# Sums over partitions by a product with ones, and another order of work at the start of both norms

## The chip, the cores and the metric

The kernel runs on one core of a Trainium2 chip. What is measured is the device time of one execution in microseconds (us), taken as the median of several executions. The engines are named as in the profile: PE (matrix products), ACT, DVE, POOL, and SP, which here only issues DMAs. Each engine works through its own queue in order, and the engines meet at semaphores.

## The reference

Two transformer blocks follow each other on a sequence of 2048 rows of 1024 values.

- Block 1: layer norm of x, product with `w_in` (1024 x 2560), three mixers (a spatial gate, a convolution of width 31, attention in a window of 128), product with `w_out`, a residual and a layer norm.
- Block 2: RMS norm, product with `w_in_2` (1024 x 4096), rotary embedding of queries and keys, three dilated windows of attention mixed by their log-sums, a short convolution, gates, product with `w_out_2`, RMS norm and a residual.

```python
x = layer_norm(x, ln_in_g, ln_in_b);   h = einsum('bsd,de->bse', x, w_in)
ya, yb, yc = spatial_gating(...), conformer_conv(...), window_attention(...)
x = layer_norm(ALPHA * x + concat(ya, yb, yc) @ w_out, post_ln_g, post_ln_b)
h = rmsnorm(x, norm_pre_g_2);          z = einsum('bsd,de->bse', h, w_in_2)
y = concat(dilated_attention(q, k, v) * silu(g), conv(...)) @ w_out_2
x = x + rmsnorm(y, norm_post_g_2)
```

## The kernel before, in words

The products with `w_in` and `w_in_2` are made in float16 with each operand split into a high and a low part, three products per pair (`products`, L164). The normed and transposed input of a block lies in SBUF whole, as `xh` and `xl`. The weights come in chunks of 256 columns: 11 in block 1, 16 in block 2. The class `Weights` (L173) takes a chunk through these steps, with two buffers of each kind:

- `sp_load` (SP): DMA of the chunk into `raw`, once the chunk two before it has been split (`ready`) and read (`read`).
- `act_sum` (ACT, L225): the sum of squares of each partition. The squares themselves are thrown away; they are written into `hi`, and so ACT waits until the chunk two before is spent.
- `pool_scale` (POOL, L230 to L243): the sum over the partitions by `partition_all_reduce`, a maximum, the power -1/2, and the factors made of it.
- Then the split: for the first chunks (`fast`) `act_hi` (L247) and `dve_lo` (L251), for the others `act_scale` (L256) on ACT and `pool_split` (L260, L262) on POOL.

The stages of a block share these weights. `norm_stage` (L286) runs at the start of each block (tag a, tag b) and makes the first three chunks' products. Its 16 row tiles come in four groups g of four. Its order is written out by hand in the list `work`, which every engine walks through: `turn` g is PE's 32 transposes (L439), ACT's scaling out of PSUM (L476), POOL's cast to `xh` (L613) and DVE's `xl` (L565); `scale` g+1 is the fetch of the next four tiles (L370), their moments on DVE (L378), a power on POOL (L427) and the scaling on DVE (L400, L402); `load` n is a chunk's sum and, if it is fast, its split; `group` n g is the product of chunk n with group g, two PSUM banks of it. On SP the load of chunk 2 stands ahead of the fetch of group 1.

For values (`fv` and `n` chunks of the norms) and for queries and keys (`rope_stage`, L1560) a bound on the results is needed too: `dve_bound` reduces the chunk's largest weights (L525, L1613), `pool_bound` (L534, L1621) sums over the partitions, `dve_fit` (L540, L1627) makes the factor that ACT's read of the result waits for. `dve_widest` and `pool_widest` (L406, L410) find the largest gain over all partitions once in each norm.

After the norm, block 1 has `conv_stage` and `spatial_stage`, block 2 has `rope_stage` and `gate_stage` (L1701). In them chunk n+1 is prepared while PE works on chunk n, whose 8 tiles (one PSUM bank each) are numbered m % 8. ACT sums at the chunk's start and scales after one group (conv, spatial) or at m % 8 == 3 (rope, gate). The stages of attention between and after them (`window_stage`, `project_stage`, `dilated_stage`) are not touched. `Banks.take` hands the eight PSUM banks (six in the conv stage) out in turn, and each taker waits for the reader of the last use.

Of the kernel before, what the change touches and what calls it, by code (L numbers as in the profile page):

```python
# [7 lines left out]
FH = mybir.dt.float16  # L8
# [49 lines left out]
def two_block_program(nc, A, out, ctx, stack):  # L58
    pe, act, dve, pool, sp = (Engine(e) for e in (nc.tensor, nc.scalar, nc.vector, nc.gpsimd, nc.sync))
    named, spare, handed, serial = {}, {}, {}, itertools.count()  # L60
    KEPT = ("c_first", "c_rest", "g_set", "w_in0", "w_in1", "a_n", "g_u", "a_w", "d_w", "g_w", "ow0", "ow1")
# [78 lines left out]
    un, us = sb("un", [128, 2, 16]), sb("us", [128, 2, 16])  # L140

    c_first, c_rest, g_set = sem("c_first"), sem("c_rest"), sem("g_set")
    FIRST, REST = (c_first, 48), (c_rest, 128)
    POWER = (g_set, 1)
# [17 lines left out]
    nc.gpsimd.memset(power[:], -0.5).then_inc(*g_set.up())  # L162

# [9 lines left out]
    class Weights:  # L173
# [3 lines left out]
        def __init__(self, tag, scope, w, chunks, block):  # L177
# [9 lines left out]
            self.dma, self.a_n, self.g_u = sems("w_in", 2), sem("a_n"), sem("g_u")  # L187
# [3 lines left out]
            self.scaled = [(self.g_u, self.g_u.n + 7 * n + 7) for n in range(len(chunks))]  # L191
# [28 lines left out]
        def act_sum(self, n):  # L220

            act.wait_ge(*self.landed[n])
            if n > 1:
                act.wait_ge(*self.spent[n - 2])
            nc.scalar.activation(self.hi[n % 2][:], self.raw[n % 2][:], ACT.Square, accum_out=self.size[:, n, 0:1]).then_inc(*self.a_n.up())  # L225

        def pool_scale(self, n):
            one, total, root, by = self.size[:, n, 0:1], self.size[:, n, 1:2], self.size[:, n, 2:3], self.size[:, n, 3:4]
            pool.wait_ge(*self.summed[n])
            nc.gpsimd.partition_all_reduce(total, one, 128, bass.bass_isa.ReduceOp.add).then_inc(*self.g_u.up())  # L230
            pool.wait_ge(*self.g_u.now())
            nc.gpsimd.tensor_scalar(total, total, 1e-30, None, ALU.max).then_inc(*self.g_u.up())
            pool.wait_ge(*self.g_u.now())
# [11 lines left out]
        def act_hi(self, n):  # L245
            act.wait_ge(*self.scaled[n])
            nc.scalar.activation(self.hi[n % 2][:], self.raw[n % 2][:], ACT.Identity, scale=self.size[:, n, 3:4]).then_inc(*self.a_w.up())  # L247
# [10 lines left out]
        def pool_split(self, n):  # L258
            pool.wait_ge(*self.by_act[n])
            nc.gpsimd.tensor_copy(self.hi[n % 2][:], self.raw[n % 2][:]).then_inc(*self.g_w.up())  # L260
# [25 lines left out]
    def norm_stage(tag, scope, src, gain, shift, gain_ready, x_ready, late, xh, xl, keep, wts, outs, heads, ones):  # L286
# [8 lines left out]
        g_pw, g_one, g_bd = sem("g_pw"), sem("g_one"), sem("g_bd")  # L295
        d_bd, d_vs = sem("d_bd"), sem("d_vs")
        vt, vh = heads
        d_wd, d_gs, g_wd, g_xh = sem("d_wd"), sem("d_gs"), sem("g_wd"), sem("g_xh")
# [4 lines left out]
        wts.widened = d_gs.at(2)  # L303
# [2265 lines left out]
```

## Time and profile before

| | us |
|---|---|
| Median of 3 runs (lowest to highest) | 2485.16 (2481.81 to 2493.55) |
| The profiled execution | 2490.25 |
| Its span in the profile | 2488.1 |
| PE busy in the span | 2093.7 (84%) |
| DVE busy | 1439.9 (58%) |
| ACT busy | 900.3 (36%) |
| POOL busy | 892.9 (36%) |

The stages, read from where their lines start and end: norm a 0 to 218, conv 218 to about 504, spatial to about 626, window attention and projection to 1024, norm b to 1241, rope to 1490 on PE, gate to about 1770, then the dilated attention with the last projection. The share of busy time is a mean over these; the waits of one stage are read from its own rows. "issue" as a releaser means that the engine waited for nothing that the profile shows.

### The profile page before, as it was taken

Reading aid. Unit: us, or ns where it says so; the run is one execution under the profiler, and the core shown is the slowest. Engines: PE = TensorE matmul, PEld = TensorE weight load, DVE = VectorE, ACT = ScalarE, POOL = GpSimd, SP = SyncE. Lnnn points to the kernel's source line nnn. Section 1 sums busy time; section 2 is a strip of 40 time slices with the busy share of each in tenths; the row PEclk is TensorE's granted clock in tenths of the full one; section 3 lists DMA queues with packets and bytes.
Section 4 is the critical chain, followed back from the end, with each engine's and each line's share of the span. In section 5 each row is a group of like instructions: output and inputs, shape, how many; then the busy total and the mean of one; then the engine's idle time right before and its main releaser. Section 6 shows DMA issues by size and latency. Waiting matters only on the chain.

```text
span 2488.1 us, 43133 instructions
## 1 busy us (share of the span) xinstructions
PE 2093.7 (84%) x16150; PEld 1540.2 (62%) x16150; DVE 1439.9 (58%) x3510; ACT 900.3 (36%) x1933; POOL 892.9 (36%) x1015
## 2 busy tenths in 40 slices
PE   2789999888588799449899999999787787776898
PEld 1444777777478688349744444747676666665776
DVE  3732877946699444465256774222198888894421
ACT  2322222221578100123223332222088787783111
POOL 2212112145141799322122131222125667873222
PEclk8899999989799899779999999999999988897999
DMA  4333131124860333222244432211267765664443
GB/s 119 111 94 119 51 123 33 45 69 144 207 146 28 127 106 114 93 93 87 73 152 115 131 113 79 68 51 52 71 160 173 171 158 151 153 191 136 144 142 108
DMA packets 285630, 279.93 MB, mean 113 GB/s; under 512 B 39936, under 2 KB 237952, under 8 KB 285168
## 3 DMA queue, kind: packets, MB, share of 16 engines
q1 hardware_dynamic: 279200, 270.01, 37.6%
q0 software_dynamic: 1680, 5.51, 0.6%
q10 hardware_dynamic: 4544, 1.66, 0.4%
q8 instruction: 129, 2.11, 0.4%
q14 instruction: 77, 0.63, 0.1%
HBM read 171.22 MB, written 93.31 MB: 106 GB/s over the span
## 4 chain that ended last, share of the span: by engine, by line
PE 41%; DVE 22%; issue 11%; POOL 11%; DMA 7%; SPq 4%; ACT 3%; DVEq 0%; ACTq 0%; POOLq 0%
PE bank L170 37%; DVE bank L843 4%; DVE s2m L2163 3%; DVE p2l L2169 3%; DMA qr<-qf 2%; SPq L1689 2%; POOL cm L2041 1%; DVE qf L1659 1%; DVE qr L1657 1%; PE bank L439 1%; POOL qs L2209 1%; DVE s2sl L1662 1%; ACT s2sh L1641 1%; POOL kept L2045 1%; POOL kept L2043 1%
## 5 line engine op out<-in xcount | busy, mean ns | idle before, releaser
L2106 PE MATMUL bank<-ident,p2r 128*128 128x128 f32 x900 | 172.0, 306 | 89.9 <-DVE p2l L2169 86.2
L170 PE MATMUL bank<-xh,w2h 128*128 128x512 f16 x640 | 243.3, 380 | 3.6 <-POOL w2l L262 3.6
L170 PE MATMUL bank<-xh,w2l 128*128 128x512 f16 x640 | 243.2, 380 | 0.0
L170 PE MATMUL bank<-xl,w2h 128*128 128x512 f16 x640 | 243.2, 380 | 0.0
L170 PE MATMUL bank<-w2h,xh 128*128 128x256 f16 x768 | 211.2, 275 | 24.9 <-issue 16.7
L170 PE MATMUL bank<-w1h,xh 128*128 128x256 f16 x768 | 214.5, 279 | 10.7 <-DVE s1st L833 10.7
L170 PE MATMUL bank<-w1l,xh 128*128 128x256 f16 x768 | 214.3, 279 | 0.0
L170 PE MATMUL bank<-w1h,xl 128*128 128x256 f16 x768 | 214.0, 279 | 0.0
L170 PE MATMUL bank<-w2l,xh 128*128 128x256 f16 x768 | 211.2, 275 | 0.0
L170 PE MATMUL bank<-w2h,xl 128*128 128x256 f16 x768 | 211.0, 275 | 0.0
L2169 DVE SCALAR_TENSOR_TENSOR p2l<-bank,p2h 128x512 f16<-128x512 f32 (+1 forms) x288 | 164.2, 570 | 48.8 <-ACT p2h L2135 48.3
L2106 PEld LDWEIGHTS bank<-ident,p2r 128*128 128x128 f32 x900 | 103.7, 152 | 138.7 <-DVE p2l L2169 136.8
L843 DVE SCALAR_TENSOR_TENSOR bank<-ain,cw,bank 128x512 f32<-128x512 f32 x240 | 181.2, 755 | 14.2 <-ACT bank L794 7.1
L2163 DVE CUSTOM_DVE_ANT_0 s2m<-bank,both,finv 128x256 f32<-128x256 f32 (+1 forms) x384 | 160.4, 455 | 9.0 <-PE bank L2096 8.7
L2135 ACT ACTIVATE p2h<-bank 128x512 f16<-128x512 f32 (+1 forms) x288 | 143.9, 500 | 28.3 <-PE bank L2106 22.9
L2142 ACT ACTIVATE p2r<-s2m,ob 128x128 f32<-128x128 f32 (+1 forms) x384 | 147.2, 434 | 8.2 <-DVE ob L2163 8.2
L170 PE MATMUL bank<-xh,w1h 128*128 128x512 f16 x320 | 122.7, 384 | 24.5 <-issue 18.2
L2124 PE MATMUL bank<-v,p2h 128*128 128x65 f16 (+1 forms) x1800 | 130.4, 201 | 0.2 <-DVE p2l L2169 0.2
L2124 PEld LDWEIGHTS bank<-v,p2h 128*128 128x128 f16 x1800 | 122.7, 103 | 5.8 <-issue 0.3
L170 PE MATMUL bank<-xl,w1h 128*128 128x512 f16 x320 | 122.8, 384 | 0.0
L170 PE MATMUL bank<-xh,w1l 128*128 128x512 f16 x320 | 122.4, 383 | 0.0
L2124 PE MATMUL bank<-v,p2l 128*128 128x65 f16 x900 | 119.1, 199 | 0.0
(328 smaller groups left out, 5521.3 us busy)
## 6 DMA issues: line engine op xcount, KB each, us to landing
scr_part<-ob SPq DMA_DIRECT2D x48, 264.0 KB, 2.9
cm<-scr_part SPq DMA_DIRECT2D x48, 264.0 KB, 4.6
w2r<-in_w_in SPq DMA_DIRECT2D x12, 1024.0 KB, 6.4
qr<-qf SPq DMA_DIRECT2D x192, 64.0 KB, 2.0
v<-scr_v SPq DMA_DIRECT2D x176, 65.0 KB, 2.2
ax<-in_x SPq DMA_DIRECT2D x16, 512.0 KB, 5.2
xr<-in_x SPq DMA_DIRECT2D x16, 512.0 KB, 4.4
bx<-scr_x SPq DMA_DIRECT2D x16, 512.0 KB, 6.3
```

The source lines that it names most:

```text
L170: ins = nc.tensor.matmul(dst, x, y, start=k == 0 and m == 0, stop=k == n - 1 and m == 2)
L439: ins = nc.tensor.transpose(bank[:, 128 * t:128 * t + 128], xs[t][:, 128 * k:128 * k + 128], ident[:])
L843: nc.vector.scalar_tensor_tensor(total[:], ain[:, 512 * q + m:512 * q + m + 512], cw[:, c, m:m + 1], total[:], ALU.mult, ALU.add).then_inc ...
L1641: nc.scalar.activation(stored(m, hbuf[m % 2]), taken(m, qf[m % 3]), ACT.Copy).then_inc(*a_qh.up())
L1657: nc.vector.tensor_tensor(r[:], r[:], sinT[:, c:c + 512], ALU.mult).then_inc(*d_rp.up())
L1689: nc.sync.dma_start(qr[m % 2][p:p + 32, :], qf[m % 3][p ^ 32:(p ^ 32) + 32, :]).then_inc(*r_in[m % 2].up(16))
L2106: ins = nc.tensor.transpose(bank[:, w * hh + 128 * c:w * hh + 128 * c + 128], p[:, hh, 128 * c:128 * c + 128], ident[:])
L2124: ins = nc.tensor.matmul(bank[:, c0:c0 + n], a[:, pc], vt[:, x["v0"] + c, vc], start=c == 0 and m == 0, stop=c == nk - 1 and m == 2)
L2135: nc.scalar.activation(pth[u % 3][:, 0:2 * x["w"]], x["t"][0][:, 0:2 * x["w"]], ACT.Copy, scale=PSCALE).then_inc(*a_ph.up())
L2142: nc.scalar.activation(pr[u % 4][:, hh, 0:w], sm[u % 3][:, hh, 0:w], ACT.Exp, bias=row[:, 130 + hh:131 + hh], scale=-1.0).then_inc(*a_ex.up())
L2163: nc.vector.tensor_tensor_reduce(sm[u % 3][:, hh, 0:w], x["s"][0][:, 256 * hh:256 * hh + w], mask_of(x), finv[:, x["j"] // 2:x["j"] // 2 + ...
L2169: nc.vector.scalar_tensor_tensor(ptl[u % 3][:, 0:w], x["t"][0][:, 0:w], PSCALE, pth[u % 3][:, 0:w], ALU.mult, ALU.subtract).then_inc(*d_pl ...
```

## The change: what it does

- A tile `ones` (128 x 128, float32) is set at the start. Every sum over partitions becomes a float32 product of `ones` with one column, on PE into a PSUM bank of its own. There are 27 for the chunks (`pe_total`), 10 for the bounds (`pe_bound`) and 2 for the gains. No `partition_all_reduce` is left. DVE reads the chunk totals (`dve_total`), and `pool_scale` waits for that.
- The squares go to a tile `junk`; the waits for the spent chunk move to the split.
- The widest gain is no longer a maximum but the root of a sum of squares. In norm a it is found after the first tiles' moments, in norm b ahead of them.
- In both norms' `work`: the split of chunk 1 stands after the moments of group 1, chunk 2 is summed at group 1 and split ahead of the last group of chunk 1. SP issues chunk 1's load at once, and the fetch of group 1 ahead of chunk 2's load.
- In the other stages, chunk n+1's total stands after the second tile of chunk n, and ACT's scaling one group (conv, spatial) or one tile (rope, gate) later.

```diff
         def act_sum(self, n):
             act.wait_ge(*self.landed[n])
-            if n > 1:
-                act.wait_ge(*self.spent[n - 2])
-            nc.scalar.activation(self.hi[n % 2][:], self.raw[n % 2][:], ACT.Square, accum_out=self.size[:, n, 0:1])...
+            act.wait_ge(*self.a_n.now())
+            nc.scalar.activation(self.junk[:], self.raw[n % 2][:], ACT.Square, accum_out=self.size[:, n, 0:1])...
+
+        def pe_total(self, n, bank, before):
+            pe.wait_ge(*self.summed[n])
+            pe.wait_ge(*ONES)
+            pe.wait_ge(*before)
+            nc.tensor.matmul(bank[:, 0:1], ones_[:], self.size[:, n, 0:1], start=True, stop=True)...
+
+        def dve_total(self, n, bank):
+            dve.wait_ge(*self.added[n])
+            nc.vector.tensor_scalar(self.size[:, n, 1:2], bank[:, 0:1], 1e-30, None, ALU.max)...

         def pool_scale(self, n):
-            pool.wait_ge(*self.summed[n])
-            nc.gpsimd.partition_all_reduce(total, one, 128, bass.bass_isa.ReduceOp.add)...
-            nc.gpsimd.tensor_scalar(total, total, 1e-30, None, ALU.max)...
+            pool.wait_ge(*self.total[n])
...
-        work = [("load", 0)]
+        work = [("wide",), ("load", 0)]
         for g in range(4):
             work.append(("turn", g))
             if g == 0:
-                work.append(("load", 1))
+                work += [("load", 1), ("total", 1)]
             if g < 3:
                 work.append(("scale", g + 1))
+            if g == 0:
+                work.append(("split", 1))
             if g > 0:
                 work.append(("group", 1, g - 1))
                 if turned:
                     work.append(("turn_v", g - 1))
             work.append(("group", 0, g))
-        work += [("load", 2), ("group", 1, 3)]
+            if g == 1:
+                work += [("load", 2), ("total", 2)]
+        work += [("split", 2), ("group", 1, 3)]
...
-        work += [("consts",), ("load", 3)]
+        work += [("consts",), ("load", 3), ("total", 3)]
...
         def sp_program():
             sp_fetch(0)
             take_over(sp)
             wts.sp_load(0)
+            wts.sp_load(1)
             for item in work:
-                if item[0] == "load":
+                if item[0] == "load" and item[1] > 1:
                     wts.sp_load(item[1] + 1)
                 elif item[0] == "scale":
                     sp_fetch(item[1])
+                    if item[1] == 1:
+                        wts.sp_load(2)
...
         # rope_stage, PE (gate_stage: the total alone)
+                if m == 0:
+                    pe_bound(0)
+                if m % 8 == 1:
+                    wts.pe_total(first + x["n"] + 1, *total_bank[x["n"]])
+                if m % 8 == 7 and x["n"] < 5:
+                    pe_bound(x["n"] + 1)
```

## Rows read from the trace of the kernel before

**Rows 1.** The page's first part, busy us of each engine.

```profile
PE 2093.7 (84%) x16150; PEld 1540.2 (62%) x16150; DVE 1439.9 (58%) x3510; ACT 900.3 (36%) x1933; POOL 892.9 (36%) x1015
```

**Rows 2.** Windows of norm a: from:to, length, PE, PEld, DVE, ACT, POOL busy, clock, DMA.

```profile
59.00:80.60 21.60, 1.37 (x7) 0.40 (x5) 11.02 (x20) 2.58 (x2) 2.83 (x7) 0.65 0.09 37
80.60:137.00 56.40, 56.31 (x301) 33.27 (x302) 40.69 (x69) 22.21 (x32) 19.20 (x22) 0.95 0.43 145
```

**Rows 3.** Timeline of norm a's start: start, length, instruction, idle before and releaser.

```profile
11.72 0.17 DVE L514 SCALAR_TENSOR_TENSOR most<-gT 128x8 f32<-128x8 f32 x1 [11.72 <-DMA bT<-in_ln_in_b]
...
18.09 0.16 DVE L386 TENSOR_SCALAR rs_in<-amv 128x4 f32<-128x4 f32 x1
...
20.59 1.05 POOL L427 TENSOR_TENSOR rs_in<-rs_in,power 128x4 f32<-128x4 f32 x1 [7.71 <-issue]
21.75 2.98 DVE L400 TENSOR_SCALAR ax<-ax,mu_in,rs_in 128x1024 f32<-128x1024 f32 x4 [2.85 <-POOL rs_in L427]
...
27.62 0.40 POOL L230 PARTITION_ALL_REDUCE w1z<-w1z  x1 [5.98 <-issue]
35.27 0.25 POOL L232 TENSOR_SCALAR w1z<-w1z 128x1 f32<-128x1 f32 x1 [7.24 <-issue]
...
37.42 2.19 POOL L613 CAST xh<-af 128x512 f16<-128x512 f32 x3
...
48.13 0.58 PE L170 MATMUL bank<-xh,w1h 128*128 128x512 f16 x1 [18.21 <-issue]
```

**Rows 4.** SP and DVE timelines between the first and second group of norm a.

```profile
52.12 2.58 SPq L370 DMA_DIRECT2D ax<-in_x  x4
...
68.16 2.35 DVE L251 SCALAR_TENSOR_TENSOR w1l<-w1r,w1z,w1h 128x2048 f16<-128x2048 f32 x1 [18.60 <-ACT w1h L247]
```

**Rows 5.** Chain of waits in norms a and b: start, length, what. x192 is two groups.

```profile
80.69 6.17 PE bank L439 x32
86.86 10.36 PE bank L170 x48
...
1103.28 5.19 PE bank L439 x32
1108.48 20.96 PE bank L170 x192
1129.43 3.49 PE bank L439 x32
```

**Rows 6.** DVE and POOL timelines of norm b's start.

```profile
1030.37 0.17 DVE L393 TENSOR_SCALAR brs<-brs 128x4 f32<-128x4 f32 x1
...
1038.76 1.05 POOL L427 TENSOR_TENSOR brs<-brs,power 128x4 f32<-128x4 f32 x1 [11.23 <-issue]
...
1052.97 0.25 POOL L232 TENSOR_SCALAR w2z<-w2z 128x1 f32<-128x1 f32 x1 [6.94 <-issue]
```

**Rows 7.** Waits by pair, PE for split weights: us in total, times, longest.

```profile
PE bank L170 <- DVE w1l L251: 6.3, 1, 6.3
...
PE bank L170 <- DVE w2l L251: 8.2, 1, 8.2
```

**Rows 8.** Rope and gate: ACT timeline; ACT's sum and DVE's bound of chunk 9.

```profile
1251.90 0.69 ACT L1600 ACTIVATE qf<-bank,qfit 128x512 f32<-128x512 f32 x1 [0.98 <-PE bank L170]
...
L225 ACT ACTIVATE w2h<-w2r x1: 1893/1893/1893, 1465.5 to 1465.5; 128x2048 f16<-128x2048 f32 x1
...
L1613 DVE TENSOR_REDUCE qwm<-w2r x1: 2284/2284/2284, 1455.8 to 1455.8; 128x8 f32<-128x2048 f32 x1
...
1514.79 1.91 ACT L225 ACTIVATE w2h<-w2r 128x2048 f16<-128x2048 f32 x1 [3.64 <-DMA scr_k2l<-s2sl]
```

**Rows 9.** PE timeline at the start of gate's second chunk.

```profile
1535.23 0.39 PE L170 MATMUL bank<-xh,w2h 128*128 128x512 f16 x1 [3.65 <-POOL w2l L262]
...
1537.05 0.63 PE L170 MATMUL bank<-xl,w2h 128*128 128x512 f16 x1
```

**Rows 10.** Float32 products with a 128 x 128 matrix (L753, eight of them): min/median/max ns.

```profile
L753 PE MATMUL bank<-brev,flip x16: 486/488/742, 296.8 to 344.5; 128*128 128x384 f32 x16
```

More of the change, by code:

```diff
@@ L190, in __init__ @@
             self.summed = [(self.a_n, self.a_n.n + n + 1) for n in range(len(chunks))]
-            self.scaled = [(self.g_u, self.g_u.n + 7 * n + 7) for n in range(len(chunks))]
+            self.added = [(self.p_t, self.p_t.n + n + 1) for n in range(len(chunks))]
+            self.total = [(self.d_t, self.d_t.n + n + 1) for n in range(len(chunks))]
+            self.scaled = [(self.g_u, self.g_u.n + 5 * n + 5) for n in range(len(chunks))]
             self.landed, self.by_act, self.half, self.ready = [], [], [], []
@@ L430, in pe_program @@
             for item in work:
-                if item[0] == "turn":
+                if item[0] == "wide":
+                    bank, before = wide_bank
+                    pe.wait_ge(*ONES)
+                    pe.wait_ge(*before)
+                    pe.wait_ge(*d_wd.at(2))
+                    nc.tensor.matmul(bank[:, 0:1], ones_[:], own, start=True, stop=True).then_inc(*p_wd.up())
+                elif item[0] == "total":
+                    wts.pe_total(item[1], *total_bank[item[1]])
+                elif item[0] == "turn":
                     g = item[1]
@@ L550, in dve_program @@
         def dve_program():
-            dve_most()
-            dve_widest()
+            if not keep:
+                dve_most()
+                dve_widest()
+                dve_widened()
             dve_scale(0)
+            if keep:
+                dve_widened()
             take_over(dve)
             for item in work:
-                if item[0] == "load" and 0 < item[1] < 3 and wts.chunks[item[1]]["fast"]:
+                if item[0] == "total":
+                    wts.dve_total(item[1], total_bank[item[1]][0])
+                elif item[0] == "split":
                     wts.dve_lo(item[1])
@@ L680, in conv_stage @@
                 if g == 1:
+                    work.append(("total", first + n + 1))
+                if g == 2:
                     work.append(("scaled", first + n + 1))
@@ L809, in dve_program @@
             for at, item in enumerate(work):
-                if item[0] == "conv":
+                if item[0] == "total":
+                    wts.dve_total(item[1], plan[at][0])
+                elif item[0] == "conv":
                     _, c, i = item
@@ L934, in spatial_stage @@
                 if n == 0 and g == 1:
+                    work.append(("total", first + 1))
+                if n == 0 and g == 2:
                     work.append(("scaled", first + 1))
@@ L1726, in gate_stage @@
                     tiles.append(x)
+                    if len(tiles) % 8 == 2 and first + n + 1 < len(wts.chunks):
+                        total_bank[n] = bk.take(wts.total[first + n + 1])
             wts.spent[first + n] = p_mm.at(len(tiles))
         def pe_program():
-            for x in tiles:
+            for m, x in enumerate(tiles):
                 bank, before = x["bank"]
@@ L1758, in dve_program @@
         def dve_program():
-            for x in tiles:
+            for m, x in enumerate(tiles):
                 bank, what, k, c = x["bank"][0], x["what"], x["k"], x["c"]
+                if m % 8 == 2 and x["n"] in total_bank:
+                    wts.dve_total(first + x["n"] + 1, total_bank[x["n"]][0])
                 s = 512 * (x["i"] % 4)
```

164 lines of the change are left out of this document (107 added, 57 removed).

## The prediction

> **What bounds the kernel now.** I read the page's busy shares first: PE has 84% of the span, more than any other engine [rows 1]. So time is lost where PE sits idle, and time added to PE counts only where it is full. The windows then show where it idles: in norm a, 59 to 80.6, PE does 1.37 us of work in 21.6, and from 80.6 on it is full [rows 2]. Norm b has the same shape [rows 5]. Third, the timeline of the start: PE's first dense product begins at 48.13 [rows 3] and the second group's transposes at 80.69; from there the products follow without a hole at 10.36 us per group of a chunk [rows 5]. What happens before 80.69, and before 1103.28 in norm b, is a chain of latencies on POOL, DVE and SP, and it ends in PE. Rope and gate are the contrary: there PE is full, and the others lag behind it [rows 8].
>
> **Norm a, first dense product.** DVE waits for the load of bT until 11.72 and starts the moments behind it; they end at 18.09 [rows 3]. In the new order the moments come first and wait for x alone. x was issued ahead of bT, the moments last 18.1 - 12.3 = 5.8, and I take them to end at 12.3 (bounds: 12.0, and 18.1 if x lands last). The power (1.05) then finds POOL free, where it stood behind the reduction until 20.59 [rows 3]. Beside it DVE makes the gain's bound and PE the product: about 1.8 us from the moments to the scaling, so 14.1, scaled at 17.1 where it was 24.73: 7.6 gained. PE's transposes, casts and `xl` follow at the old pace, but without the hole: POOL idled 5.98 before the reduction, ran 0.40, idled 7.24 behind it, and the first cast came at 37.42 [rows 3]. New: transposes 17.1, two casts by 21.2, total and `pool_scale` (five small operations, 35.6 to 37.4 before) by 24.1, ACT's split, six casts and DVE's `xl` with `dve_lo` between them (10.7 us from 37.4 to 48.1 before, less what two early casts save) end at about 32.1. First dense product at 32.1: 16.0 earlier.
>
> **Norm a, second group.** Before, SP issued the fetch at 52.12, behind chunk 2's load, which waits for the split of chunk 0; then DVE waited 18.60 for chunk 1's split and did it ahead of the moments [rows 4]. Now the fetch goes when the transposes end (22.5), lands by 29, and the moments follow the bound of chunk 0: start 33.7, end 39.5, power 40.8, scaled 43.8. PE is busy with group 0 of chunk 0 until 32.1 + 10.4 + 1.8 (half clock at its start) = 44.3. So both arrive together. DVE still has to split chunk 1 (2.4) and make the fit (0.7) before it frees the banks that the last transposes take: they end at 49.0 instead of 86.86 [rows 5]: 37.9 gained. The next wait in line is then PE's own work.
>
> **Norm a, the rest.** The wait for chunk 2's split, 6.3 [rows 7], and 1.9 of half clock behind it go (1.2 GHz, the lower level, as after the idle 59 to 80.6 with 0.65 [rows 2]): its sum comes at group 1 and its split under 10.4 us of products. New are two waits. `pe_total` of chunks 2 and 3 stands directly behind a group's last product, while ACT's sum stands behind the read of that product: 0.69 + 1.9 and the hops, 3.2 each, and queued behind the waiting PE are transposes that everybody needs. A stall of 3.65 was followed by matmuls of 0.63 instead of 0.39, half the clock [rows 9]; that cost about 1.6. So 2 x 4.8 = 9.6 (bounds 5 and 12). Sum for norm a: 37.9 + 8.2 - 9.6 - 0.5 for products = 36.
>
> **Norm b.** Here the gains' bound stays ahead of the moments, now with a PE and a POOL hop: the moments end 2.8 later than 1030.5, at 1033.3. But the power stood at 1038.76 after 11.23 of POOL's idleness [rows 6] and now follows at once, 5.4 earlier, and the scaling and PE's transposes with it (1037.3 instead of 1042.7, four us behind the power as before). The idle 6.94 and its partner ahead of the reduction go [rows 6]. The old first dense product I put at 1065.7, since the one in norm a came 12.8 behind the maximum on POOL [rows 3, 6]; the new one, 15 behind the transposes as in norm a, at 1052.3. From there as in norm a, with a bound over a whole chunk more on DVE (2.7): second transposes end at 1073.9 instead of 1108.48 [rows 5]: 34.6. Chunk 2's wait 8.2 [rows 7] and 2 of clock go, 2 x 4.8 come, 0.5 products: 35.
>
> A statement of the Trainium skill speaks against this part: GPSIMD Engine Reference, section When to use GPSIMD, names the reduction across partitions as work for which POOL is the only option. By that only the reordered loads would gain, since the reduction is busy for just 0.40. This trace disagrees: the 13 idle us round each one are what its 0.40 costs here.
>
> **The price of a product.** A float32 product of one column is not in the trace. Above: L753 is two instructions of 488 ns for 384 columns, so at most 1.0 [rows 10]. Below: nothing, where PE would idle anyway. I take 0.3, since most of those 488 is columns. 39 products; where PE is full 20 of them count, 6 us (0 to 20), part of the stage sums here.
>
> **Conv and spatial.** The totals come 10 us after the chunk's start and find ACT's sum done. Conv's second half waits for DVE's taps, to which `dve_total` adds 0.15 each. +1.5. In spatial the reduction held up POOL's first power; that gives back about 3 (bounds -6 and +2). The later scaling still leaves over 8 us before the chunk is needed.
>
> **Rope and gate.** Here it costs. PE ended tile 1 at 1251.9 and makes a tile in 5.18. Tile 39 thus ended at 1448.7, but DVE's bound for the next chunk ended at 1455.8 + 2.3 + 0.4 = 1458.5 [rows 8]. It did not matter, because the reader of the result waited, not PE. Now PE itself waits there with the next chunk queued behind: at every chunk's end PE is held to where DVE is, and its lead is gone. Summed: rope ends on PE at 1458.5 + 0.2 + 8 x 5.18 + 0.3 = 1500.4, which was 1448.7 + 41.4 = 1490.2. The readers do not lose, they were behind. But the gate stage used this lead: PE did its first chunk while ACT still stored. Its first sum begins at 1514.79 and takes 1.91 [rows 8], with its read 1516.9, PE arrives at the total at 1510.8, waits 6.1, and ends the chunk at 1517.2 + 31.1 + 1.6 + 0.3 = 1550.2. Before it began the second chunk at 1535.23 after the wait of 3.6 [rows 9], with its own 1.6 of clock. Lost: 13.4, and 1.6 for later products: 15 (bounds 4, if the bounds do not hold PE, and 28).
>
> **Sum.** -36 - 35 + 1.5 - 3 + 15 = -57.5. Against the profiled execution's 2490.25 that is 2432.7; this execution lies 5.1 above the median of 2485.16, so the forecast is 2427.7, say 2428.
>
> **Rivals.**
> (A) PE keeps its lead in rope: the lag of the bounds shrinks because DVE is less held up. For it: DVE's long operations there fall together with POOL's split, which moves. Against: the order in DVE is unchanged. Then 13 of the 15 stay: 2415.
> (B) The second group stays exposed. Transposes would start some 12 us later in each norm, because x lands late or PE, POOL and DVE hand over slower than I chained them. For: my chain has twenty hops. Time 2428 + 24 = 2452. The change not doing what it says ends near there too: if POOL's idle time belongs to the powers and not to the reductions, 2 x 13 us stay, 2454. Against that: the 6 and 7 us stand on both sides of each reduction, and the casts behind a power have none [rows 3].
> (C) Slower: PE's queue becomes the lock. Each total and bound behind the norms waits for a full sum or reduction, and the readers then wait for PE: 19 totals x (1.9 + 0.7 + 1.6 + 0.3) = 86 and 5 bounds x 4.9 = 25. 2485 - 71 - 3 + 111 = 2522. It decides from an average of 3 us per product behind the norms (74 / 25). Against: in conv and gate ACT is idle at those points.
> (D) No change that can be told: B and a third of C together, 24 + 37 against 57.5.
>
> **How the numbers follow.** Forecast 0.60, A 0.12, B 0.20, C 0.05, D 0.03. About 0.5% (12 us) is what a measurement of this kernel tells from no change. Own range of the forecast: openings +-12, rope and gate -11 to +13, products -6 to +14, spatial +-4, of which not all fall together: 2408 to 2446. With A and B taken in: 2404 to 2458. C and D are left out. Faster by over 0.5%: 0.92; within 0.03; slower 0.05.
>
> **What would show it.** First dense product at 31 to 35; second transposes of norm a ending at 47 to 55, of norm b at 1074 less norm a's shift. A PE wait of about 3 before the transposes of group 2 in each norm, none for L251. In rope, PE idle in small pieces at each chunk's end, in gate one wait of some 6 for L225. No idle POOL time of 6 to 8 before small operations. It would be wrong if x lands after 40, if a product costs 1 us, or if ACT in rope waits for PE.

## The result, and the profile after

The changed kernel takes 2420.7 us (median of 4 runs, 2416.8 to 2428.2) against 2489.4 of the kernel before in the same comparison (4 runs, 2481.8 to 2497.7): ratio 0.973, 95% interval 0.968 to 0.977. That is 68.6 us less; 2428 was forecast. Its profiled execution took 2428.2 (span 2426.4), 62.0 less than the profiled one of before. Single executions of one kernel differ by 11 us here (changed) and 16 us (before), so below a stage is compared by marks within the profiles, and the whole by medians. The profiled execution of the changed kernel is the slowest of its four.

The page's busy shares after; they answer to [rows 1]. POOL's busy time fell by 28.8 only (892.9 before), so most of what went was not POOL's work:

```profile
PE 2106.3 (87%) x16228; PEld 1550.3 (64%) x16228; DVE 1433.8 (59%) x3539; ACT 902.4 (37%) x1933; POOL 864.1 (36%) x956
```

The same two stretches as in [rows 2] (length, then busy time of PE, PEld, DVE, ACT and POOL, PE's granted clock, DMA share, GB/s). In 59 to 80.6, where PE had done 1.37 us of work, it now does 18.93:

```profile
59.00:80.60 21.60, 18.93 (x100) 11.46 (x99) 13.36 (x23) 10.20 (x14) 7.96 (x13) 0.92 0.53 149
80.60:137.00 56.40, 53.86 (x272) 26.97 (x269) 28.99 (x42) 17.88 (x25) 10.26 (x11) 1.00 0.33 110
```

The timeline of norm a's start (start, length, engine, line, what; in brackets the idle time before it and what ended it) answers to [rows 3, 4]. Moments end at 11.85, the power has no idle time behind a reduction, the wide gain passes PE in 0.74, and chunk 0's scalars (L246 to L254) follow DVE after 0.88 where 5.98 and 7.24 stood. The fetch goes at 22.55, ahead of chunk 2's load:

```profile
4.84 1.29 DVE L406 BATCH_NORM_STATS2 ast<-ax 128x6 f32<-128x512 f32 x2 [4.84 <-DMA ax<-in_x]
11.69 0.16 DVE L414 TENSOR_SCALAR rs_in<-amv 128x4 f32<-128x4 f32 x1
11.94 1.02 POOL L463 TENSOR_TENSOR rs_in<-rs_in,power 128x4 f32<-128x4 f32 x1 [10.95 <-DVE rs_in L414]
12.74 0.56 PE L472 MATMUL bank<-wide,ones 128*128 128x1 f32 x2 [12.74 <-DVE wide L438]
13.33 0.16 DVE L440 TENSOR_SCALAR wide<-bank 128x1 f32<-128x1 f32 x1 [0.74 <-PE bank L472]
13.42 2.98 DVE L429 TENSOR_SCALAR ax<-ax,mu_in,rs_in 128x1024 f32<-128x1024 f32 x4
21.15 0.57 POOL L246 TENSOR_TENSOR w1z<-w1z,power 128x1 f32<-128x1 f32 x1 [0.88 <-DVE w1z L240]
22.55 1.76 SPq L398 DMA_DIRECT2D ax<-in_x  x4
...
32.92 1.80 SPq L222 DMA_DIRECT2D w1r<-in_w_in  x3
33.20 1.28 DVE L406 BATCH_NORM_STATS2 ast<-ax 128x6 f32<-128x512 f32 x2
43.31 2.35 DVE L264 SCALAR_TENSOR_TENSOR w1l<-w1r,w1z,w1h 128x2048 f16<-128x2048 f32 x1
```

PE in norms a and b from the first dense product on: it starts at 31.80, the second transposes run from 43.67 to 48.55 with one wait of 1.01, then come a wait of 2.67 and one of 2.72 for the sums of chunks 2 and 3. (Ahead of it the product for chunk 1's total waited 7.10 for ACT's sum and went at 29.62; PE then still waited 1.59 for the operands of the dense product.) In norm b the same: 1004.31, then the second transposes to 1026.66, with a wait of 4.61 inside, then 3.11 and 2.67:

```profile
31.80 0.58 PE L172 MATMUL bank<-xh,w1h 128*128 128x512 f16 x1 [1.59 <-issue]
47.02 1.53 PE L483 MATMUL bank<-ident,ax 128*128 128x128 f32 x12 [1.01 <-DVE asl L638]
72.38 0.59 PE L236 MATMUL bank<-w1z,ones 128*128 128x1 f32 x2 [2.67 <-ACT w1j L229]
137.18 0.59 PE L236 MATMUL bank<-w1z,ones 128*128 128x1 f32 x2 [2.72 <-ACT w1j L229]
...
1004.31 0.37 PE L172 MATMUL bank<-w2h,xh 128*128 128x256 f16 x1 [1.96 <-issue]
1024.13 2.53 PE L483 MATMUL bank<-ident,bx 128*128 128x128 f32 x12 [4.61 <-DVE bvo L643]
1051.54 0.38 PE L236 MATMUL bank<-w2z,ones 128*128 128x1 f32 x2 [3.11 <-ACT w2j L229]
1115.69 0.38 PE L236 MATMUL bank<-w2z,ones 128*128 128x1 f32 x2 [2.67 <-ACT w2j L229]
```

Behind the first of these waits the clock is near the lower level, 1.2 GHz:

```profile
73.00:76.00 3.00, 3.00 (x17) 3.00 (x17) 0.54 (x2) 1.89 (x3) 2.35 (x7) 0.57 1.01 283
```

In rope and gate PE now waits where it did not ([rows 8, 9] had only the 3.65 for a split). The three longest waits for a bound or a sum there, in order, and ACT's late sum:

```profile
1168.73 0.59 PE L1712 MATMUL bank<-qbd,ones 128*128 128x1 f32 x2 [3.72 <-DVE qbd L1706]
1378.63 0.38 PE L1712 MATMUL bank<-qbd,ones 128*128 128x1 f32 x2 [2.44 <-DVE qbd L1706]
1436.36 1.91 ACT L229 ACTIVATE w2j<-w2r 128x2048 f16<-128x2048 f32 x1 [3.52 <-DMA scr_k2l<-s2sl]
1438.41 0.59 PE L236 MATMUL bank<-w2z,ones 128*128 128x1 f32 x2 [5.75 <-ACT w2j L229]
```

How much earlier than in the kernel before a mark of each stage comes, in the profiles of all the kernels (worked out from their timelines; the marks are ACT's last read in norm a, conv's last read for a tap, the first softmax read of window attention, the last read of the projection behind it, rope's first and last reads, the gate's last read, and the span's end):

| kernel | norm a | conv | att. start | proj. end | rope start | rope end | gate end | span | median us |
|---|---|---|---|---|---|---|---|---|---|
| changed | 37.2 | 36.1 | 44.0 | 48.3 | 80.0 | 77.5 | 63.6 | 61.7 | 2420.7 |
| e_norm_pool | 14.3 | 13.4 | 20.7 | 26.9 | 38.8 | 43.1 | 29.1 | 31.0 | 2461.6 |
| e_old_order | 29.0 | 27.2 | 35.0 | 38.6 | 67.7 | 69.3 | 56.4 | 57.0 | 2433.0 |
| e_fetch_late | 26.8 | 25.9 | 33.5 | 37.3 | 64.2 | 63.9 | 51.1 | 53.9 | 2436.0 |
| e_order_rest | 31.6 | 30.5 | 38.3 | 41.7 | 69.4 | 68.9 | 56.2 | 59.3 | 2428.6 |
| e_spatial_pool | 37.2 | 36.1 | 34.3 | 44.0 | 76.1 | 76.8 | 63.1 | 62.1 | 2430.0 |
| e_rope_gate_pool | 37.2 | 36.2 | 43.9 | 48.0 | 81.3 | 81.2 | 83.7 | 85.1 | 2404.6 |
| e_norm_late | 45.6 | 44.6 | 52.0 | 55.6 | 98.2 | 99.4 | 86.7 | 86.4 | 2403.6 |
| e_rope_late | 36.9 | 35.9 | 43.7 | 49.4 | 81.0 | 74.9 | 74.0 | 74.7 | 2415.5 |
| e_both_late | 45.6 | 44.3 | 51.8 | 58.2 | 98.0 | 90.7 | 89.8 | 89.8 | 2402.9 |
| e_gate_late | 46.0 | 44.0 | 51.7 | 55.8 | 98.0 | 98.0 | 91.5 | 92.5 | 2398.2 |
| e_sum_early | 45.8 | 44.9 | 51.6 | 53.9 | 93.6 | 100.2 | 98.8 | 97.8 | 2390.6 |
| e_norm_rope | 45.7 | 44.3 | 52.2 | 56.0 | 98.4 | 98.7 | 101.2 | 96.9 | 2391.5 |

The medians of the kernel before, beside these runs, are 2489.4, 2488.3, 2487.1 and 2489.4, so medians may be compared across the table, though a difference of 5 or 8 us between two of them is within the scatter of single executions (up to 16 us in these two kernels). Stages whose code is the same also differ between profiles: from rope's first to its last read the kernels with the changed kernel's rope range from 2.5 us longer to 4.3 us shorter than before.

### The profile page after: what moved, and what is told of

Read it like the earlier page. It is cut to its first block, busy times and chain, and to the rows that moved or that the text cites. A ratio compares the mean times of both kernels' runs of the same rounds, so it can differ in the third digit from the quotient of the medians.

```text
span 2426.4 us, 43240 instructions
## 1 busy us (share of the span) xinstructions
PE 2106.3 (87%) x16228; PEld 1550.3 (64%) x16228; DVE 1433.8 (59%) x3539; ACT 902.4 (37%) x1933; POOL 864.1 (36%) x956
## 3 DMA queue, kind: packets, MB, share of 16 engines
q8 instruction: 130, 2.13, 0.4%
## 4 chain that ended last, share of the span: by engine, by line
PE 24%; DVE 11%; POOL 8%; issue 3%; DMA 3%; ACT 2%; SPq 2%; DVEq 0%; ACTq 0%; POOLq 0%
PE bank L172 23%; DVE s2m L2261 4%; DVE p2l L2267 3%; POOL cm L2139 1%; POOL qs L2307 1%; POOL gt L2147 1%; DMA qr<-qf 1%; DVE qf L1752 1%; POOL kept L2143 1%; POOL kept L2141 1%; SPq L1781 1%; DVE qr L1750 1%; POOL kept L2139 1%; ACT s2sh L1732 1%; POOL yo L2492 1%
## 5 line engine op out<-in xcount | busy, mean ns | idle before, releaser
L912 DVE SCALAR_TENSOR_TENSOR bank<-ain,cw,bank 128x512 f32<-128x512 f32 x240 | 181.2, 755 | 14.2 <-ACT bank L861 7.1
L2233 ACT ACTIVATE p2h<-bank 128x512 f16<-128x512 f32 (+1 forms) x288 | 143.9, 500 | 28.8 <-PE bank L2204 23.2
L246 POOL TENSOR_TENSOR w2z<-w2z,power 128x1 f32<-128x1 f32 x16 | 9.1, 568 | 406.8 <-DVE w2z L240 358.2
```

The source lines that it names most:

```text
L912: nc.vector.scalar_tensor_tensor(total[:], ain[:, 512 * q + m:512 * q + m + 512], cw[:, c, m:m + 1], total[:], ALU.mult, ALU.add).then_inc ...
L2233: nc.scalar.activation(pth[u % 3][:, 0:2 * x["w"]], x["t"][0][:, 0:2 * x["w"]], ACT.Copy, scale=PSCALE).then_inc(*a_ph.up())
```

## Experiments

The theory: POOL's reduction costs the norms some 13 us of idleness each time and the products remove it; the order of loads adds less; and a product makes PE wait in its queue, which costs in the norms' second half and in rope and gate. The chief rival: the new order makes the gain, and the products are incidental.

### Which part gives the gain in the norms

**e_norm_pool**: the changed kernel with the reduction back for totals 0 to 3 and the bounds of both norms.

```diff
         def pe_total(self, n, bank, before):
+            if n in self.pooled:
+                return
...
         def pool_scale(self, n):
+            if n in self.pooled:
+                pool.wait_ge(*self.summed[n])
+                nc.gpsimd.partition_all_reduce(total, self.size[:, n, 0:1], 128, bass.bass_isa.ReduceOp.add)...
...
+                nc.gpsimd.tensor_scalar(total, total, 1e-30, None, ALU.max)...
...
-        wts = Weights("w1", sc, A["w_in"][0], chunks1, 0)
+        wts = Weights("w1", sc, A["w_in"][0], chunks1, 0, range(4))
```

> The changed kernel's order of work is kept, but in both norms the totals of the first four chunks and the bounds are again made by POOL's reduction over partitions; the gain's own bound stays a product. My theory: each reduction costs POOL about 13 us of idleness (6 before, 7 behind it), and up to the second group's transposes two of them stand on the chain (first total and first bound; each norm). So the first dense product of norm a starts at about 44 instead of 31, the second group's transposes end near 70 instead of 49, norm b the same, and the time rises by about 44 us to 2464. Rival (the order of loads, squares and scales alone makes the gain in the norms): at most 5 us more, about 2425, and the idle time around the reductions lies beside other work.

Measured: 2461.6, ratio 0.989 (0.988 to 0.991). 40.9 more than the changed kernel; 44 said, 5 by the rival. The first dense product starts at 45.36 (44 said) and the second group's transposes end at 70.4 (70 said), where the changed kernel has them at 48.55. POOL's timeline shows how it happens: idleness before and behind, and a reduction that directly follows another shares it:

```profile
50.11 0.40 POOL L601 PARTITION_ALL_REDUCE abd<-abd  x1 [6.00 <-issue]
50.43 0.46 POOL L258 PARTITION_ALL_REDUCE w1z<-w1z  x1
58.36 0.25 POOL L260 TENSOR_SCALAR w1z<-w1z 128x1 f32<-128x1 f32 x1 [7.47 <-issue]
```

At the end of ACT's last read of group 1 the two kernels are 21.3 apart in norm a (53.5 and 74.8) and 41 apart in norm b, as much as the medians differ. (The spans of the two profiles differ by 30.7 only; nearly 7 of the 41 are lost again in rope, whose code is the same in both.) Behind that point the experiment has a flaw of its own: I left the bank of chunk 2's total reserved, so the last transposes of group 2 wait for the total, 8.61 in norm a and 9.92 in norm b; the waits of PE for sums, which this kernel doesn't have, weigh about as much on the other side. The openings themselves are free of it. So their chain of waits is the reductions', and most of the norms' gain with it.

**e_old_order**, **e_fetch_late** and **e_order_rest**: products stay, the order of the norms goes back, wholly or one of its two parts.

```diff
 # e_fetch_late (and in e_old_order), SP:
-                    sp_fetch(item[1])
                     if item[1] == 1:
                         wts.sp_load(2)
+                    sp_fetch(item[1])
 # e_order_rest (and in e_old_order), the list of work:
             if g == 0:
-                work += [("load", 1), ("total", 1)]
+                work += [("load", 1), ("total", 1), ("split", 1)]
             if g < 3:
                 work.append(("scale", g + 1))
-            if g == 0:
-                work.append(("split", 1))
...
-            if g == 1:
-                work += [("load", 2), ("total", 2)]
-        work += [("split", 2), ("group", 1, 3)]
+        work += [("load", 2), ("total", 2), ("split", 2), ("group", 1, 3)]
```

> The products stay everywhere, but in both norms the order of the work is the old one: chunk 2's load ahead of the fetch of group 1, chunk 1 split ahead of group 1's moments and scaling, chunk 2 summed and split ahead of the last group. My theory (products give most, order the rest): 6 to 8 us of SP order and 1 to 3 of the rest in each norm, about 16 more, 2437, with norm a's second transposes ending near 57. Rival (order is the main part): 40 more, about 2460.

> Only one thing is undone: on SP the load of chunk 2, which waits for chunk 0's split, goes again ahead of the fetch of group 1. My theory: the fetch of norm a then goes at about 32 instead of 22.5 and lands at about 38, so that moments, power and scaling come 6 to 9 later; PE is busy with group 0's products until about 42, so 7 us in each norm remain: 14 more, 2434. Rival (group 1 is hidden behind group 0's products anyway): 0 to 3 more.

> The changed kernel with the fetch of group 1 early, as it has it, but the rest of the old order in both norms: chunk 1 split ahead of the moments and scaling of group 1, chunk 2 loaded, summed and split ahead of the last group. My theory (this rest is worth little: with the late fetch it was 3 us faster than the new order): moments 2 to 3 later per norm, no wait for the split of chunk 2 since its total is still early enough, so 2 to 5 more, 2424. Rival (chunk 2's early sum is what removed the waits of 6.3 and 8.2 for its split): 12 to 16 more, 2435.

Measured: the whole old order 2433.0 (ratio 0.978, 0.976 to 0.979), 12.3 more; the late fetch alone 2436.0 (0.978, 0.976 to 0.980), 15.3 more; the rest alone 2428.6 (0.976, 0.974 to 0.978), 7.9 more. The rows below are, one kernel each, PE's longest wait before the second transposes in each, in this order, where the changed kernel waits 1.01:

```profile
51.38 5.22 PE L479 MATMUL bank<-ident,ax 128*128 128x128 f32 x32 [6.27 <-DVE ax L425]
```

```profile
54.02 6.38 PE L483 MATMUL bank<-ident,ax 128*128 128x128 f32 x32 [9.79 <-DVE ax L429]
```

```profile
49.45 6.12 PE L479 MATMUL bank<-ident,ax 128*128 128x128 f32 x32 [4.42 <-DVE ax L425]
```

The order is the smaller part: 12 us are lost without it, 41 without the products. What each is worth depends on the other. In norm a the products with the old order stand at 29.0 us ahead of the kernel before, the new order with POOL's reductions (e_norm_pool, with its flaw) at 14.3, both together at 37.2; so the order gives 8 beside the products, and the products give 23 beside the order. One part of the change was never undone by itself: that norm a's moments no longer wait for the gain and shift (moments first, `dve_widest` behind them). It is in all these kernels. I had put the late fetch right (14 said); the rest of the order I had thought worth 3 and it is 8, a difference that the executions' scatter does not settle, but the marks do (norm a 5.6 and rope's start 10.6 later). The parts don't add (15 + 8 against 12): with a late fetch, splitting chunk 1 first would fill DVE's wait for the data, so that the new place of the split pays only together with the early fetch. The marks fit this (norm a 29.0 with both old, 26.8 with the fetch alone late); no run moves the split of chunk 1 alone. No PE wait for chunk 2's split is seen in e_order_rest or e_old_order; so the earlier sum was not needed to remove the 6.3 and 8.2 of [rows 7]: with the product in the total they go in the old order too.

### Where a product makes PE wait

**e_norm_late**: in both norms totals 2 and 3 move to places where ACT's sum is done.

```diff
             work.append(("turn", g))
+            if g == 2:
+                work.append(("total", 2))
...
-                work += [("load", 2), ("total", 2)]
+                work += [("load", 2)]
...
-        work += [("consts",), ("load", 3), ("total", 3)]
-        work += [("group", 2, 0), ("scaled", 3)] + [("group", 2, g) for g in range(1, 4)]
+        work += [("consts",), ("load", 3)]
+        work += [("group", 2, 0), ("total", 3), ("group", 2, 1), ("scaled", 3)] + [("group", 2, g) for g in range(2, 4)]
```

> In both norms the product for chunk 2's total moves behind the transposes of group 2, and chunk 3's behind the first group of chunk 2 (its scaling one group later): at those places ACT's sum is done when PE arrives. My theory: PE's waits of 2.67 and 2.72 for the sums go, and with them the half clock behind each (1.3 and 1.7): 8.4 per norm, 17 together, about 2404. Rival (the wait only shows a lateness of the readers behind it, so that PE then waits for the transposes' banks or ACT instead): 0 to 5 less, 2416 to 2421.

Measured: 2403.6 (ratio 0.966, 0.964 to 0.969), 17.1 less than the changed kernel; 17 said. In norm a 8.4 are gained, and from the projection's end to PE's last work in norm b 9.1. No wait for a sum of chunk 2 or 3 is left, and the stretch behind total 2, which had a clock of 0.57, has full clock:

```profile
73.00:76.00 3.00, 2.77 (x15) 1.38 (x14) 1.67 (x2) 2.79 (x5) 2.77 (x4) 1.00 1.03 266
```

**e_rope_gate_pool**: POOL's reduction again for the totals of chunks 4 to 15 of block 2 and for rope's bounds.

> The totals of the second block's chunks from 4 on (rope and gate) and rope's bounds are made by POOL's reduction again; the norms keep the products. My theory (PE's lead in rope was lost at the bounds, and then the gate's first total made it wait 5.8): 15 us are given back, about 2406, with no PE wait at the gate's start but the old one of 3.6 for chunk 2's split back. Rival (only the products' own time and their small waits count): 6 less, about 2414. Second rival (readers bound rope, so that nothing changes): 0.

Measured: 2404.6 (0.966, 0.964 to 0.968), 16.1 less. The gate keeps all of rope's shift (81.2 and 83.7), where the changed kernel lost 13.9 between them. So the products in rope and gate cost what the forecast had for them, and with the norms' gain the change would be faster without them. The wait of 3.6 for a split did not come back at its old place; PE waits 1.03, 1.41 and 0.33 for POOL's splits late in rope and at the gate's start.

**e_rope_late** and **e_both_late**: instead of going back to POOL, products at other places; the second with the norms' later ones.

```diff
 # rope
-                if m == 0:
-                    pe_bound(0)
                 if m % 8 == 1:
+                    pe_bound(x["n"])
+                if m % 8 == 3:
                     wts.pe_total(first + x["n"] + 1, *total_bank[x["n"]])
-                if m % 8 == 7 and x["n"] < 5:
-                    pe_bound(x["n"] + 1)
...
 # gate
-                if m % 8 == 1 and x["n"] in total_bank:
+                if m % 8 == (1 if x["n"] else 5) and x["n"] in total_bank:
...
```

The parts of DVE and ACT that belong to a moved product move with it (ACT's scaling in the gate only).

> All sums stay products, but in rope each bound's product stands behind the second tile of the chunk that it is for, instead of behind the last tile of the chunk before, each total's behind the fourth tile, and the gate stage's first total behind the sixth. My theory (PE was held at each bound to where DVE was, and so met the gate's first sum too late): PE keeps its lead, the gate's first wait goes, 13 to 15 less, about 2406, as with POOL's reductions. Rival (products as such cost this, not where they stand): 0 to 3 less, 2418 to 2421. Second rival (readers now get the bound two tiles later, ACT is late at each chunk's first tile): 5 x 3 more, 2436.

> Both moves together: the norms' products for totals 2 and 3 later, and rope's and the gate's first ones later. My theory: both gains add, since they lie in different stages: 17 + 15 = 32 less than the changed kernel, about 2389, the fastest of all. Rival (a lead gained in one place is lost at the next transfer or queue): 2400 to 2405.

Measured: e_rope_late 2415.5 (0.971, 0.969 to 0.973), 5.3 less where 15 was said, and e_both_late 2402.9 (0.966, 0.963 to 0.968), no more than the norms alone gave, where 2389 was said. The waits for bounds and for the gate's sum are gone, and the gate loses only 0.9. But rope now loses 6 to 7 of its shift: PE waits for POOL's split at five chunks' starts, which I put down to the total behind the fourth tile, since it makes the next chunk's scaling and split late. PE's waits in rope and the start of gate in e_rope_late (us in total, times, longest):

```profile
PE bank L172 <- POOL w2l L277: 10.2, 5, 3.4
```

I had moved a wait, not removed it. Two things follow for rope: its totals must not move back, and what is late is the sum that they wait for.

**e_gate_late**: e_norm_late and only the gate's first total later.

> The norms' later products for totals 2 and 3 (2404 in all) and one move more: the gate stage's first total, its product behind the sixth tile instead of the second, DVE's and ACT's parts with it. Rope is as in the changed kernel. My theory: the wait of 5.8 for ACT's sum at the gate's start and what follows from it is a loss of 12 to 14 by itself; without it the gate keeps rope's shift, so 12 less, 2391. Rival (the gate lost through the lead that the bounds took, so PE is then held elsewhere): 0 to 4 less, 2400 to 2404.

Measured: 2398.2 (0.964, 0.963 to 0.966), 5.4 less than e_norm_late where 12 was said. Between rope's and the gate's end 6.5 are lost instead of 12.7. So the wait of 5.1 seems worth about its own length; the single executions of the two kernels overlap (2395 to 2408 and 2397 to 2405), so this rests on the marks. The other half I put down to PE's lead, gone in rope at the bounds (waits of 2.13 and 2.44 are still there).

**e_sum_early**: the norms as in e_norm_late; in rope and gate ACT makes the sum of squares two tiles earlier, and the bounds stand behind the second tile of their own chunk.

```diff
 # rope, ACT (the gate in the same way, without its sum at m == 0)
-                if m % 8 == 0:
-                    wts.act_sum(first + m // 8 + 1)
+                if m == 0:
+                    wts.act_sum(first + 1)
+                if m % 8 == 6:
+                    wts.act_sum(first + m // 8 + 2)
 # rope, PE
-                if m == 0:
-                    pe_bound(0)
                 if m % 8 == 1:
+                    pe_bound(x["n"])
                     wts.pe_total(first + x["n"] + 1, *total_bank[x["n"]])
-                if m % 8 == 7 and x["n"] < 5:
-                    pe_bound(x["n"] + 1)
```

> The norms as in the run of 2404. In rope and gate ACT makes each chunk's sum of squares ahead of the seventh tile of the chunk two before it, instead of ahead of the first tile of the chunk before it; the products for totals keep their place behind the second tile, rope's bounds stand there too. So no product there finds its sum or bound unready, and the scaling is not made later. My theory: rope loses neither the 2 to 3 per chunk that PE waited for splits when the totals stood behind the fourth tile, nor the gate's 12: 2390. Rival (ACT is what paces the end of rope, and a sum in its place costs as much as anywhere): 2396 to 2400. Second rival (readers get their bound two tiles later and that decides): 2403.

Measured: 2390.6 (median of 4, 2386.3 to 2392.2; ratio 0.9605, 0.959 to 0.962); 2390 said. Rope's first read comes 4.6 later against the kernel before than in e_norm_late (93.6 and 98.2), since its bound now stands two tiles later, and this costs PE nothing. The run moves two things, the sums and the bounds; beside e_both_late, which has the bounds at the same place, it shows that the totals' place and the earlier sums are worth 12, but the earlier sums alone were not run. From 1150 to 1400 PE has no idle time and full clock:

```profile
1150.00:1400.00 250.00, 250.00 (x1174) 115.01 (x1173) 173.50 (x234) 89.78 (x112) 53.56 (x42) 1.00 0.44 130
```

**e_norm_rope**: the norms' later products, and POOL's reductions for rope and gate.

> The norms' later products, and POOL's reductions again for rope and gate. My theory: the two gains (17 and 16) lie in different stages and add: 2388. Rival (rope's readers were the bound in the norms' run already): 2395 to 2403.

Measured: 2391.5 (0.9603, 0.959 to 0.962); 2388 said. Beside the norms' 17 it gives 12 more, of the 16 that it gave alone. Well placed products and POOL's reductions are the same there within the error: where POOL has slack its idleness is nearly free (PE waits 2.4 us in all for its splits), and so is a product that finds its operand ready.

### Spatial

**e_spatial_pool**: only the total of the chunk that the spatial stage scales is POOL's again.

> One total alone is POOL's reduction again: that of the chunk which the spatial stage sums and scales. The stage gained 7.9 to 8.7 us where I had forecast 3. My theory (the 12 us round the reduction held up POOL's first power in the stage, and with it what its readers need): the stage is 6 to 9 longer again, total about 2428. Rival (the later scaling or the stage's other order makes the gain): 0 to 1 more, 2421.

Measured: 2430.0 (0.978, 0.975 to 0.980), 9.3 more than the changed kernel. From conv's mark to the start of attention it takes 9.7 longer, 174.7, where the kernel before took 172.9; so the new order without the product gains nothing here. The stage hangs on a chain that goes back and forth between DVE and POOL, and POOL's first multiplication of `mv` stands right behind the scalars (480.46 in the changed kernel, 494.68 here). POOL's last one comes 9.8 later, so 4.4 of the 14.2 are made up on the way. The reduction and the idleness round it, in e_spatial_pool:

```profile
484.56 0.40 POOL L258 PARTITION_ALL_REDUCE w1z<-w1z  x1 [5.74 <-issue]
492.51 0.25 POOL L260 TENSOR_SCALAR w1z<-w1z 128x1 f32<-128x1 f32 x1 [7.55 <-issue]
```

In this one profile attention and projection give 5.4 of it back and the span ends where the changed one's does; by medians the 9.3 stay. A single pair of spans does not decide between them.

## Why the prediction was right

**Norm a, first dense product.** Said 32.1, measured 31.80. Moments said to end at 12.3: 11.85. The parts that I took from [rows 3] (casts, split, `xl`) keep their lengths. Undoing the norms' products moved it to 45.36.

**Norm a, second group.** Said transposes ending at 49.0, measured 48.55; fetch said at 22.5, went at 22.55. That load order and reduction both stood on this chain is shown by e_fetch_late (wait of 9.79 there, transposes ending at 60.40) and e_norm_pool (70.4).

**The new waits.** Said 3.2 each and 1.6 of clock, 4.8 together; measured 2.67, 2.72, 3.11 and 2.67, and e_norm_late gives 17.1 for the four with their clock, 4.3 each. The 6.3 and 8.2 for chunk 2 went, though not for the reason that I gave: I put it to the early sum, and the old order has no such wait either. Norm a gained 37.2, said 36.

**Norm b.** Dense product said 1052.3; 1004.31 plus the 48.3 by which all is earlier there is 1052.6. Transposes said 1073.9, measured 1026.66 + 48.3 = 1075.0. From the end of project to PE's last work in norm b 33.3 are gained, said 35.

**The price of a product.** Said 0.3. The profile lists each as two products and two weight loads (x32 for 16). One whose operand is ready costs PE less than forecast: around the one at 1482.99 the dense products start 0.36 apart where their neighbours start 0.22 apart, so 0.14; the other ready products between dense ones cost the same. In none of the runs is it what decides; where it stands is. Below, durations in ns (lowest, median, highest), then PE's timeline:

```profile
L236 PEld LDWEIGHTS bank<-w2z,ones x32: 186/190/338, 990.5 to 1649.9; 128*128 128x128 f32 x32
L236 PE MATMUL bank<-w2z,ones x32: 167/250/373, 990.7 to 1649.9; 128*128 128x1 f32 x32
...
1482.56 0.38 PE L172 MATMUL bank<-xl,w2h 128*128 128x512 f16 x1
1482.77 0.38 PE L172 MATMUL bank<-xh,w2l 128*128 128x512 f16 x1
1482.99 0.28 PE L236 MATMUL bank<-w2z,ones 128*128 128x1 f32 x2
1483.13 0.38 PE L172 MATMUL bank<-xh,w2h 128*128 128x512 f16 x1
```

**Conv and spatial.** Conv said 1.5 lost, measured 1.1 at this mark. Spatial is the term that was mis-sized: said 3 gained, measured 7.9. That lies outside its bounds (6 gained at most). I had counted only POOL's first power as held up; but POOL's multiplications of `mv` stand behind the scalars too, and DVE and POOL wait for each other from there on. With the reduction back the first of them is 14.2 later and the stage 9.7 longer (e_spatial_pool).

**Rope and gate.** Said 15 lost, as PE being held at the bounds and then meeting the gate's sum too late with a wait of 6.1. Measured: from rope's first read to the gate's last 16.4 lost, the wait 5.75, and e_rope_gate_pool gives back 16.1. On PE itself rope, from its first product to the gate's first, takes 262.5 where it took 248.6: about 14 more, 10.2 said; with POOL's reductions it takes 251.4. The split between the two causes was right in kind: e_gate_late gives 5.4 for the gate's wait, and the rest comes back only where the bounds move too. In all seven kernels that have both products at the changed kernel's places, the gate loses 12.7 to 14.0 between its marks.

Three details were wrong. The largest wait for a bound came at the first one (3.72; directly behind it, from 1168 to 1175, the clock is 0.52), for which the forecast had nothing; in other kernels with the same rope it is 2.1 (2.14 in e_norm_late) or again 3.9 (e_order_rest, e_spatial_pool). The later ones are 0.64 and 2.44, less than the lag of [rows 8] says; that PE had no lead left to lose by then is my reading. And I had written that the readers do not lose, and that ACT waiting for PE in rope would be a sign of being wrong. That sign is there: 21.4 us in 13 times for ACT's `qf`, where before it was 1.0 once. The readers' last mark in rope comes 2.5 later for it against the first, which is within what rope varies between these profiles, so the step failed but the sum hardly felt it.

**Rivals.** A (the lead is kept, 2415) is excluded by the waits and not by the time, since 2420.7 lies between the two. B (the second group exposed, or the idleness not the reductions') is excluded by e_norm_pool and the 48.55, C and D by the time.

**Unforecast.** Window attention and projection are together 4.3 shorter, though the change does not touch them: attention by itself is 4.9 shorter, the projection 0.6 longer. It is so in every kernel with the change (4.0 to 5.1 for attention, 10.1 in e_spatial_pool), and its cause stays open; the last section has one candidate.

**Sum.** By profiles the span is 61.7 less, 57.5 said. Norm a gave 1 more than said, spatial 5 more, attention and projection 4 where nothing was said; norm b gave 2 less, rope with its first bound and the gate 3 less, and behind the gate another 1.9 are lost for which the forecast had nothing; conv is right to 0.4. By medians the gain is 68.6, so 11 more than said. The places and waits were right; that the total comes so near is in part luck, since some stages gave 10 us more and others 7 less than said, and 4.3 of the gain has nothing to do with the theory.

The best version is e_sum_early: 2390.6, 30.1 below the changed kernel, and its interval (0.959 to 0.962) lies apart from the changed kernel's (0.968 to 0.977). It keeps POOL free of reductions; e_norm_rope is as fast.

## What to carry to other kernels

A one-word sum over partitions costs by what its engine does around it: before putting it on another engine look for idleness in front of and behind the small instruction, not at its length. Put on PE it becomes a wait in the queue of the engine that bounds the kernel, so it belongs behind work that is long enough for its operand to be ready. Moving it back is enough where its result is not needed soon (17 in the norms). In rope it made the next consumer late (10.2 of waits for splits), and there the version with an earlier operand was the fast one. Of a change with several edits undo each by itself; the two order edits here were worth 12 together and 15 and 8 alone.

## What the runs showed of the hardware

POOL's reduction has 0.40 of work. Where POOL waited for nothing else that the profile shows, 5.7 to 6.1 of idleness stand before it in nearly all the norms and in spatial, and more elsewhere. Before the next ordinary instruction at least 6.7 stand behind it, mostly 7 to 9, in 63 of 64 places in the traces; once, in e_norm_pool, a cast followed after 1.98. Two directly in a row paid it once (50.11 and 50.43 above), but in rope, where the second had to wait for its operand, some 7 to 9 lay between two reductions as well. The traces show this idleness but not what fills it. What stands before agrees in size with the Trainium skill, GPSIMD Engine Reference, section Instruction dispatch, which gives approximately 6 us (5.95 measured) that the first call to a freshly loaded kernel pays, with no instruction visible in the profile. What stands behind is longer still here.

A wait of 2.7 on PE was followed by 3 us at a clock of 0.57, near its lower level of 1.2 GHz. Without the four waits of 2.7 to 3.1 the kernel was 17.1 shorter, so each cost about 4.3 (e_norm_late).

A small DVE addition of two SBUF operands, 0.16 in the median, took 2.35 when it began beside a POOL subtraction of 2.36, and ended with it. In the profile of the kernel before, DVE's and POOL's timelines:

```profile
711.33 2.35 DVE L1327 TENSOR_TENSOR mx<-sink,mx 128x8 f32<-128x8 f32 x1
...
711.30 2.36 POOL L1367 TENSOR_TENSOR wol<-woR,woh 128x1024 fp32r<-128x1024 f32 x1
```

The Trainium skill, SBUF — State Buffer, section SBUF: two separate sides, says that a DVE operation with two SBUF inputs and a POOL operation that reads SBUF exclude each other for the whole instruction, and that the one that starts first gets through; this row agrees (POOL began 0.03 earlier). It happened twice there, and twice more in part (0.75 and 0.48); after, twice in part (0.43 and 0.28). The mean of this instruction fell from 0.49 to 0.19, 4.9 us over its 16, as much as attention got shorter. But the other kernels do not follow: in e_gate_late the mean is 0.37 and attention 4.2 shorter, in e_spatial_pool 0.39 and 10.1. So that this made attention shorter is not shown.
